# Two halves of a weight in one tile, word by word, and the moving rows at another distance

## The chip, the core and the metric

The kernel runs on one core of a Trainium2 chip, as one launch. The metric is the device time of that launch in microseconds. TensorE (PE in the profile) multiplies, and loads its stationary operand with an instruction of its own (PEld in the profile); VectorE (DVE) and ScalarE (ACT) do the elementwise work, SyncE (SP) issues the transfers of the weights.

## The reference, cut to what matters

Two layer blocks run one after the other on 256 positions of width 2048, in float32. Nearly all of the work is a chain of matrix products with large weights, each weight read once:

```
proj = rmsnorm(h) @ w_in + b_in             # 2048 x 11272, then mLSTM and a causal convolution
h = h + (gates * branches) @ w_out          # 2048 x 2048
u = causal_dwconv(rmsnorm(h) @ w_up)        # 2048 x 11008
h = h + (silu(gate) * val) @ w_down         # 5504 x 2048
# second block, on 16 + 256 positions:
proj = rmsnorm(h) @ w_in_2                  # 2048 x 10240, then pooling, a gated recurrence, gelu
h = h + merged @ w_out_2
h = h + square(relu(rmsnorm(h) @ mlp_w1)) @ mlp_w2   # 2048 x 8192 x 2048
out = rmsnorm(h)
```

## The kernel before, in words

**Products in three parts.** TensorE works here on the type float32r, which keeps fewer bits of a number than float32. So each weight is split in two: a high half (the weight written as float32r, `whi`) and a low half (the weight less its high half, `wlo`). The activations are split in the same way: the tiles `hn` (normalised rows) and `act` (other operands) hold for each of the 16 feature tiles the high part in columns 0 to 255 of the row and the low part behind it. A product of a 128 x 128 block of weights and 256 positions is three matmuls into the same bank of PSUM: high times high, high times low, low times high (L461 to L463). The weights are the stationary operand, the activation rows are the moving one, so each of the three matmuls is preceded by a load of 128 columns of weights.

**The weight stream.** SyncE brings the weights in chunks of 4 x 512 columns per partition (1 MB in all) into a ring `raw` of four. Each chunk is split as two halves of 1024 columns. For each half ScalarE copies raw to a slot of `whi` (L727), VectorE subtracts (L1040) into the same slot of `wlo`, and TensorE runs 24 matmuls on it: 2 rows of tiles, 4 column tiles, 3 parts. There are 4 slots. Half n+4 may be written when the 24 matmuls of half n are done (`half_used`), and the two engines keep their program order three halves ahead (`AHEAD`). All other work of ScalarE and VectorE (moving sums out of PSUM, gates, convolutions, splits of the activations) stands between these splits in an order fixed by hand (`stream`). Everything is ordered by semaphores; there is no scheduler. 952 halves pass through in all.

**The wide stages.** In `lru_in` and `pool_in` of the second block the moving rows are 272 columns (16 extra positions), and the low part comes from the tile `lo2` (L485 to L487, in `group_wide`).

**Where the tiles lie.** The tiles are laid out in each partition in the order of allocation: `raw` (32 KB), `whi` (16 KB), `wlo` (16 KB), `h` (16 KB), an unused `gap_a`, `hn`, `act`, and the rest. A slot of `whi` or `wlo` is 4096 bytes and a block of 128 weights 512 bytes, so every block starts at a multiple of 256 bytes from the start of `whi`. A row of `hn` is 2304 bytes, 9 times 256, and its moving part starts 256 bytes into it; a row of `act` is 2048 bytes. So every moving row of 256 columns starts, modulo 256 bytes, at the same distance from every block of weights: the 192 bytes of `gap_a`. In the wide stages `hn` is read from 64 bytes ahead of that, and the rows of `lo2` are 1088 bytes apart, so that their distance goes through four values.

Of the kernel before, what the change touches and what calls it, by code (L numbers as in the profile page):

```python
# [5 lines left out]
F32R = mybir.dt.float32r  # L6
# [5 lines left out]
P = 128  # L12
# [9 lines left out]
HALF = CK // 2 * NC  # L22
RAW = 4
SLOTS = 4
# [59 lines left out]
def build(nc, a, out):  # L84
    PH, GROUPS, CHUNKS = plan()
    ctx = ExitStack()
    with ctx:
        def sb(name, shape, dt=F32, stack=ctx):
            return stack.enter_context(nc.sbuf_tensor(name, shape, dt))
# [7 lines left out]


        raw = sb("raw", [P, RAW, CK * NC])
        whi = sb("whi", [P, SLOTS, HALF], F32R)  # L100
        wlo = sb("wlo", [P, SLOTS, HALF], F32R)
        h = sb("h", [P, NT, T])

        sb("gap_a", [P, 48])
        hn = sb("hn", [P, NT, MAIN + 2 * T], F32R)
        act = sb("act", [P, NT, 2 * T], F32R)
        meta_lo = hn[:, :, MAIN - 2 * META:MAIN - META]
# [1472 lines left out]
```

How the kernel before makes its waits and increments, by code:

```python
        @block.sync  # L313
# [7 lines left out]
            def load(c, c_slot, dst_cols, src):  # L321
                if not (isinstance(c, int) and c < RAW):
                    sp.wait_ge(lo_ready, 2 * c - 2 * RAW + 2)
                kt, n = src.shape[1], src.shape[2]
                dst = raw[:, c_slot % RAW, :].rearrange("p (k n) -> p k n", n=dst_cols)[:, 0:kt, 0:n]
                sp.dma_start(dst, src).then_inc(chunk_loaded[c_slot % RAW], 16)
# [15 lines left out]
                        load_x(j)  # L343
                    kt = min(CK, w.shape[1] - k0 - CK * j)
                    cl = s * nch + j
                    load(ph.c0 + per_body * i + cl, cl + (body * per_body if ph.unroll else 0), NC,
                         w[:, k0 + CK * j:k0 + CK * j + kt, ds(column, n)])
            for ph in PH.values():
                if ph.name == "lru_gates":
                    for q in range(4):
                        sp.wait_ge(lo_ready, 2 * (ph.c0 + q) - 2 * RAW + 2)
                        for s, w in enumerate((W_ga, W_gx)):
                            sp.dma_start(raw[:, q, s * HALF:(s + 1) * HALF].rearrange("p (k n) -> p k n", n=256),
                                         w[:, 4 * q:4 * q + 4, :]).then_inc(chunk_loaded[q], 16)
# [15 lines left out]
                    c = slice(half * D // 2, (half + 1) * D // 2)  # L372
                    for e in ("even", "odd"):
                        sp.wait_ge(sem(f"out_copied_{e}"), 2 * t + half + 1)
                    sp.dma_start(out[0, t * P:(t + 1) * P, c], out_nat[:, t, c]).then_inc(sem("out_stored"), 16)
```

## Time and profile before

| | us |
|---|---|
| median of 3 runs | 2875.09 (2865.03 to 2888.51) |
| the profiled execution | 2872.45 |
| its span, first to last instruction | 2870.7 |
| TensorE busy in it | 2744.2 (96%) |
| VectorE busy | 1711.4 (60%) |
| ScalarE busy | 1300.1 (45%) |
| mean granted TensorE clock | 0.979 of full speed |

The time is what the launch took on the device; the span is the part of it between the first and the last instruction, here 1.75 us shorter. The profiled execution lies 2.6 us under the median of the runs. TensorE's busy time is the union of overlapping matmuls, so a full share says that it was never without one, not how fast they followed each other.

### The profile page before, as it was taken

Reading aid. Unit: us, or ns where it says so; the run is one execution under the profiler, and the core shown is the slowest. Engines: PE = TensorE matmul, PEld = TensorE weight load, DVE = VectorE, ACT = ScalarE, POOL = GpSimd, SP = SyncE. Lnnn points to the kernel's source line nnn. Section 1 sums busy time; section 2 is a strip of 40 time slices with the busy share of each in tenths; the row PEclk is TensorE's granted clock in tenths of the full one; section 3 lists DMA queues with packets and bytes.
Section 4 is the critical chain, followed back from the end, with each engine's and each line's share of the span. In section 5 each row is a group of like instructions: output and inputs, shape, how many; then the busy total and the mean of one; then the engine's idle time right before and its main releaser. Section 6 shows DMA issues by size and latency. Waiting matters only on the chain.

```text
span 2870.7 us, 53265 instructions
## 1 busy us (share of the span) xinstructions
PE 2744.2 (96%) x22994; PEld 2721.2 (95%) x22994; DVE 1711.4 (60%) x1725; ACT 1300.1 (45%) x1449; POOL 1.8 (0%) x14
## 2 busy tenths in 40 slices
PE   4988999999999999999999967999999999999998
PEld 4987999999999999999989967999999999999998
DVE  4544565566667567657785648755665555455555
ACT  3443454444554355445544375444454334343443
POOL 0000000000000000000000000000000000000000
PEclk9988999999999999999999988999999999999999
DMA  4442555555555555555545424555556565655653
GB/s 154 162 146 93 195 193 192 190 191 191 187 194 180 197 182 196 198 191 165 173 165 171 154 98 132 191 185 182 190 179 189 189 182 187 191 183 185 186 183 115
DMA packets 257814, 503.17 MB, mean 175 GB/s; under 512 B 10150, under 2 KB 19038, under 8 KB 257630
## 3 DMA queue, kind: packets, MB, share of 16 engines
q1 hardware_dynamic: 254592, 500.20, 53.1%
q8 instruction: 127, 2.08, 0.3%
q10 hardware_dynamic: 3054, 0.55, 0.1%
q14 instruction: 41, 0.34, 0.0%
HBM read 498.63 MB, written 2.10 MB: 174 GB/s over the span
## 4 chain that ended last, share of the span: by engine, by line
PE 87%; DVE 7%; ACT 4%; ACTq 1%; issue 1%; DVEq 0%
PE psum L461 27%; PE psum L462 27%; PE psum L463 26%; PE psum L485 2%; PE psum L486 2%; PE psum L487 2%; DVE wlo L1040 2%; DVE work L1068 1%; DVE work L1408 1%; ACT whi L727 1%; ACTq L713 1%; DVE misc L1454 0%; ACT misc L950 0%; DVE hn L1078 0%; DVE work L1439 0%
## 5 line engine op out<-in xcount | busy, mean ns | idle before, releaser
L1040 DVE TENSOR_TENSOR wlo<-raw,whi 128x1024 fp32r<-128x1024 f32 x952 | 1160.1, 1223 | 983.6 <-ACT whi L727 982.7
L727 ACT ACTIVATE whi<-raw 128x1024 fp32r<-128x1024 f32 x952 | 1003.3, 1058 | 1317.4 <-PE psum L463 1194.3
L461 PE MATMUL psum<-hn,whi 128*128 128x256 f32 x4448 | 1249.5, 281 | 38.9 <-DVE wlo L1040 25.9
L462 PE MATMUL psum<-hn,whi 128*128 128x256 f32 x4448 | 1247.0, 280 | 0.0
L463 PE MATMUL psum<-hn,wlo 128*128 128x256 f32 x4448 | 1246.7, 280 | 0.0
L461 PEld LDWEIGHTS psum<-hn,whi 128*128 128x128 f32 x4448 | 846.1, 190 | 42.6 <-DVE wlo L1040 28.9
L463 PEld LDWEIGHTS psum<-hn,wlo 128*128 128x128 f32 x4448 | 848.7, 191 | 0.0
L462 PEld LDWEIGHTS psum<-hn,whi 128*128 128x128 f32 x4448 | 842.5, 189 | 0.1
L461 PE MATMUL psum<-act,whi 128*128 128x256 f32 x2544 | 711.8, 280 | 14.8 <-DVE wlo L1040 9.3
L463 PE MATMUL psum<-act,wlo 128*128 128x256 f32 x2544 | 711.0, 279 | 0.0
L462 PE MATMUL psum<-act,whi 128*128 128x256 f32 x2544 | 710.9, 279 | 0.0
L461 PEld LDWEIGHTS psum<-act,whi 128*128 128x128 f32 x2544 | 479.5, 188 | 16.2 <-DVE wlo L1040 9.9
L463 PEld LDWEIGHTS psum<-act,wlo 128*128 128x128 f32 x2544 | 484.9, 191 | 0.0
L462 PEld LDWEIGHTS psum<-act,whi 128*128 128x128 f32 x2544 | 479.2, 188 | 0.0
L485 PE MATMUL psum<-hn,whi 128*128 128x272 f32 x512 | 150.4, 294 | 6.5 <-DVE wlo L1040 6.5
L486 PE MATMUL psum<-lo,whi 128*128 128x272 f32 x512 | 149.2, 291 | 0.0
L487 PE MATMUL psum<-hn,wlo 128*128 128x272 f32 x512 | 148.6, 290 | 0.0
L485 PEld LDWEIGHTS psum<-hn,whi 128*128 128x128 f32 x512 | 98.1, 192 | 7.2 <-DVE wlo L1040 3.8
L487 PEld LDWEIGHTS psum<-hn,wlo 128*128 128x128 f32 x512 | 98.0, 191 | 0.0
L486 PEld LDWEIGHTS psum<-lo,whi 128*128 128x128 f32 x512 | 98.0, 191 | 0.0
L1053 DVE TENSOR_TENSOR work<-psum,scale 128x1024 f32<-128x1024 f32 (+2 forms) x58 | 70.5, 1215 | 27.2 <-PE psum L463 27.2
L1326 DVE SCALAR_TENSOR_TENSOR work<-work,cols 128x256 f32<-128x256 f32 x172 | 71.9, 480 | 1.7
(207 smaller groups left out, 978.3 us busy)
## 6 DMA issues: line engine op xcount, KB each, us to landing
raw<-in_w_in SPq DMA_DIRECT2D x160, 1024.0 KB, 5.1
raw<-in_mlp_w SPq DMA_DIRECT2D x128, 1024.0 KB, 5.3
raw<-in_w_up SPq DMA_DIRECT2D x80, 1024.0 KB, 5.0
raw<-in_w_down SPq DMA_DIRECT2D x40, 1024.0 KB, 5.1
raw<-in_w_out SPq DMA_DIRECT2D x32, 1024.0 KB, 5.0
raw<-in_w_branch_m SPq DMA_DIRECT2D x8, 1024.0 KB, 5.0
raw<-in_w_branch_c SPq DMA_DIRECT2D x8, 1024.0 KB, 5.0
raw<-in_w_up SPq DMA_DIRECT2D x8, 768.0 KB, 4.4
```

Source lines behind the costliest of these rows:

```text
L461: mm(o, hi[:, kk, w], both[:, 0, :], start=first, stop=False)
L462: mm(o, hi[:, kk, w], both[:, 1, :], start=False, stop=False)
L463: last = mm(o, lo[:, kk, w], both[:, 0, :], start=False, stop=end)
L485: mm(o, hi[:, kk, w], hn[:, kt, MAIN - META:MAIN + T], start=(kt == 0), stop=False)
L486: mm(o, hi[:, kk, w], lo2[:, kt, :], start=False, stop=False)
L487: last = mm(o, lo[:, kk, w], hn[:, kt, MAIN - META:MAIN + T], start=False, stop=(kt == NT - 1))
L713: ac.dma_start(stage[at:at + n, s, :], src).then_inc(sem("stage_loaded"), 16)
L727: A(whi[:, n % SLOTS, :], raw[:, n // 2 % RAW, n % 2 * HALF:(n % 2 + 1) * HALF], ACT.Copy)\
L1040: V.tensor_tensor(wlo[:, n % SLOTS, :], raw[:, n // 2 % RAW, n % 2 * HALF:(n % 2 + 1) * HALF], whi[:, n % SLOTS, :].bitcast(F32), ALU.subt ...
L1053: V.tensor_tensor(dst, summed(ph, i, s, tiles), over_tiles(stream_scale, tiles), ALU.mult)\
L1068: V.tensor_reduce(dst[:, ds(g, 1), :].rearrange("p o t -> p (o t)"), src.rearrange("p k t -> p t k"), AX.X, ALU.add).then_inc(sem("squares ...
L1326: last = V.scalar_tensor_tensor(up_conv[s][:, m, :], up_pad[s][:, m, k:k + T], dcol(f"ffn_w{k}", t), up_conv[s][:, m, :], ALU.mult, ALU.add)
```

## The change

One tile `wsplit` takes the place of `whi` and `wlo`, with 2048 words for each slot. `whi` and `wlo` are now views of it: the high half of weight x is word 2x, the low half word 2x+1. Nothing else in the code is touched, so ScalarE writes every second word, VectorE reads the high halves as every second word and writes the low halves to the words between, and TensorE loads 128 weights from 1024 bytes, every second word of them. The tile begins where `whi` began and takes the same 32 KB. `gap_a` goes from 192 to 64 bytes, so `hn`, `act` and all tiles behind them lie 128 bytes lower, and a moving row of 256 columns starts 64 bytes (modulo 256) from every block of weights. In the wide stages `hn` is read from 0 bytes and `lo2` from other distances than before.

```
-        whi = sb("whi", [P, SLOTS, HALF], F32R)
-        wlo = sb("wlo", [P, SLOTS, HALF], F32R)
+        wsplit = sb("wsplit", [P, SLOTS, 2 * HALF], F32R)
+        whi, wlo = [wsplit[:, :, :].rearrange("p s (x t) -> p s x t", t=2)[:, :, :, t] for t in range(2)]
         h = sb("h", [P, NT, T])
 
-        sb("gap_a", [P, 48])
+        sb("gap_a", [P, 16])
```

The instructions of every engine, their order, their sizes and their waits are the same before and after.

## Rows read from the trace of the kernel before

**Rows 1.** The page: span, TensorE, granted clock in 40 slices, last chain.

```profile
span 2870.7 us, 53265 instructions
PE 2744.2 (96%) x22994; PEld 2721.2 (95%) x22994; DVE 1711.4 (60%) x1725; ACT 1300.1 (45%) x1449; POOL 1.8 (0%) x14
...
PEclk9988999999999999999999988999999999999999
...
PE 87%; DVE 7%; ACT 4%; ACTq 1%; issue 1%; DVEq 0%
```

**Rows 2.** TensorE by stretch: bounds, length, busy (instructions), granted clock, DMA share, GB/s.

```profile
74.00:246.00 172.00, 155.00 (x1172) 0.92 0.39 129
252.00:741.00 489.00, 488.75 (x4306) 1.00 0.58 192
742.00:926.00 184.00, 184.00 (x1564) 1.00 0.56 187
929.00:1357.00 428.00, 427.34 (x3771) 1.00 0.58 190
...
1461.00:1670.00 209.00, 202.46 (x1560) 0.98 0.51 170
...
1792.00:1843.00 51.00, 51.00 (x453) 1.00 0.58 193
1848.00:2859.00 1011.00, 1009.69 (x8567) 1.00 0.57 181
```

**Rows 3.** Timeline of TensorE near 1000 us, the first and last of 28 matmuls.

```profile
999.93 0.28 PE L461 MATMUL psum<-hn,whi 128*128 128x256 f32 x1
...
1002.99 0.28 PE L461 MATMUL psum<-hn,whi 128*128 128x256 f32 x1
```

**Rows 4.** The same near 2000 us, the first and last of 28 matmuls.

```profile
1999.76 0.28 PE L461 MATMUL psum<-hn,whi 128*128 128x256 f32 x1
...
2002.94 0.28 PE L461 MATMUL psum<-hn,whi 128*128 128x256 f32 x1
```

**Rows 5.** The same in a wide stage, the first and last of 25 matmuls.

```profile
1519.90 0.29 PE L485 MATMUL psum<-hn,whi 128*128 128x272 f32 x1
...
1522.92 0.29 PE L485 MATMUL psum<-hn,whi 128*128 128x272 f32 x1
```

**Rows 6.** Timeline of TensorE, 32 matmuls of type float32, one after the other.

```profile
66.81 7.07 PE L540 MATMUL psum<-h,work 128*8 128x256 f32 x32
```

**Rows 7.** Timeline of TensorE at the end, 24 transposes of type float32.

```profile
2856.26 2.85 PE L681 MATMUL psum<-ident,h 128*128 128x128 f32 x24 [1.31 <-DVE h L1293]
```

**Rows 8.** Groups by line: busy us, mean ns of one, idle before, releaser.

```profile
L1040 DVE TENSOR_TENSOR wlo<-raw,whi 128x1024 fp32r<-128x1024 f32 x952 | 1160.1, 1223 | 983.6 <-ACT whi L727 982.7
L727 ACT ACTIVATE whi<-raw 128x1024 fp32r<-128x1024 f32 x952 | 1003.3, 1058 | 1317.4 <-PE psum L463 1194.3 <-PE psum L487 119.6 <-PE psum L646 1.9
...
L1068 DVE TENSOR_REDUCE work<-work 128x256 f32<-128x1024 f32 x24 | 47.9, 2009 | 1.1 <-ACT work L756 1.1
```

**Rows 9.** Who waited for whom: us in total, times, longest us.

```profile
ACT whi L727 <- PE psum L463: 1194.3, 722, 10.2
DVE wlo L1040 <- ACT whi L727: 982.7, 650, 5.8
...
PE psum L461 <- DVE wlo L1040: 35.3, 11, 6.6
```

**Rows 10.** Busy PE, PEld, DVE, ACT, POOL, in an up and an MLP stretch.

```profile
760.00:926.00 166.00, 166.00 (x1411) 166.00 (x1411) 115.01 (x137) 83.88 (x96) 0.00 (x0) 1.00 0.55 184
...
1848.00:2855.00 1007.00, 1006.95 (x8543) 1006.54 (x8542) 565.44 (x494) 415.91 (x405) 0.00 (x0) 1.00 0.57 182
```

**Rows 11.** DMA issues of the page: count, KB each, us to landing.

```profile
raw<-in_w_in SPq DMA_DIRECT2D x160, 1024.0 KB, 5.1
```

## The prediction

> **What bounds the kernel now.** I read the page first. The span is 2870.7 us, TensorE is busy for 2744.2 of it, the granted clock stands at full speed (2.4 GHz) nearly everywhere, and 87% of the last chain is TensorE's own work [rows 1]. In the long stretches it is never idle [rows 2]. The waits say the same from the other side: ScalarE's split waits for TensorE to free a slot for 1194.3 us in all and VectorE's for ScalarE for 982.7 us, while TensorE waited for a low half 11 times, for 35.3 us [rows 9]. So the time is a number of matmuls times the spacing at which they follow each other, and a busy share of 100% hides that spacing. It is the next thing to read.
>
> The timeline gives it. Near 1000 us 27 matmuls take 1002.99 - 999.93 = 3.06 us, 113.3 ns each [rows 3]. Near 2000 us the same instructions at the same clock, on the same tiles, take 2002.94 - 1999.76 = 3.18 us, 117.8 ns each [rows 4]. The counts by stretch show that this isn't a local matter: 252 to 741 us, 929 to 1357 and 1792 to 1843 run at the short spacing (489/4306 = 113.6 ns), 742 to 926 and 1848 to 2859 at the long one (184/1564 = 117.6, 1011/8567 = 118.0) [rows 2]. A stretch keeps its spacing for hundreds of microseconds through stages with other weights and operands, and it changes only where TensorE had to wait. A supply that is too slow would show as idle time and would not stay that even; it looks like the phase between two streams that run side by side, the moving rows and the next weights, which is set when TensorE starts again.
>
> What would be the spacing without such a loss? 32 matmuls in float32, with 256 columns, take (7.07 - 0.38)/31 = 215.8 ns each (0.38 being the last one's own length) [rows 6]. That is two passes of 256 columns at 2.4 GHz (213.3 ns) and 2.5 ns. 24 transposes of 128 float32 columns, each with its own weight load, take (2.85 - 0.27)/23 = 112 ns, the slower first one after the wait included [rows 7]; two passes of 128 are 106.7 ns. So the same array with one load for each matmul comes down to about 106.7 + 2.5 = 109.2 ns, an estimate from these two groups. Against it the three-part product loses 4.1 ns per matmul in one phase and 8.6 in the other. In the wide stage 24 matmuls take 3.02 us, 125.8 ns [rows 5], where 272 columns and 2.5 ns make 115.8: a loss of 10.0 ns, and there the distance of the rows from the weights is another.
>
> **The change part by part.** The instructions are the same, so nothing but the length of one and the spacing can change.
>
> *The weight load and the moving rows.* Before, TensorE reads 1024 bytes of moving row while it reads 512 bytes of weights: the two addresses run at two speeds and one passes the other again and again, modulo whatever length the memory is divided by. After, both walk 1024 bytes in the same 106.7 ns, at a start distance that is 64 bytes (modulo 256) for every pair of `hn` or `act` row and weight block, with low halves only one word off. If the loss comes from the two reads meeting, they can now meet once per matmul at the most and, 64 bytes apart, not at all. I take the loss as gone in the narrow stages: spacing 109.2 ns. The float32 rows are the nearest cases: in [rows 7] both streams also walk at one speed, 512 bytes each, and the loss is small or nil, though at half the rate of bytes, so it is a hint and not a proof. The other end: each block now spans twice the bytes. If meetings go by the bytes that the weight load passes over, the loss doubles, to 113.3 + 4.1 = 117.4 and 117.8 + 8.6 = 126.4 ns.
>
> Sum for the narrow stages: at the short spacing 4306 + 3771 + 453 = 8530 matmuls x 4.1 ns = 35.0 us; at the long one 1172 + 1564 + 8567 = 11303 x 8.6 = 97.2 us [rows 2]. About 1100 more (22994 less these and the 1560 wide ones, less the few hundred of other kinds) stand in the broken stretches between, some 6 us. Together 138 us.
>
> *The wide stages.* 1560 matmuls [rows 2] x 10.0 ns would be 16 us if their loss went too. But here `hn` starts 0 bytes from the weights and `lo2` at four distances, so the even distance doesn't hold. I take half, 8 us, with -16 and +16 us as ends.
>
> *The splits on ScalarE and VectorE.* ScalarE now writes every second word, VectorE reads one source and writes its output so. Bounds: at best nothing changes, 1058 and 1223 ns [rows 8]. The only access in this trace that isn't word after word is the reduction over tiles, which reads 1024 words 1024 bytes apart: 2009 ns, 786 ns over the plain 1024-word subtraction [rows 8]. A hop of 8 bytes is far nearer to 4 than to 1024, so I take 0, and keep 786 ns for one such stream and 1572 ns for two as ends. The cover is large: a half takes TensorE 24 x 113.3 = 2.72 us, there are three halves between a freed slot and its use (8.2 us), and the chain through ScalarE and VectorE is 1.06 + 1.22 = 2.3 us. Doubled it would still fit, as long as VectorE has time on average. That is the point to check. In the up stretch VectorE is busy 115.0 of 166 us for 1411/24 = 59 halves [rows 10]; 59 x 0.786 = 46 more makes 161, above the 59 x 24 x 109.2 ns = 154 us that TensorE would need. In the MLP stretch it is 565 of 1007 us for 356 halves; 280 more makes 845 against 933: it fits.
>
> Two rules of the Trainium skill speak against each other here. The Trainium skill, Vector Engine (DVE) Microarchitecture Reference, section Expressivity limits, says that a stream keeps its full rate only in runs of at least two adjacent 4-byte words, and gives 1.73 ns per column for one source that hops every word and 1.98 for all three; by it a split would take some 1.8 to 2.1 us. The Trainium skill, SBUF — State Buffer, in its remark on 16-byte cachelines, says that two hits in each line of 16 bytes are enough, which every second float32 word gives; by it nothing changes. The page with the price has no case with a hop of 8 bytes, and no row here has one.
>
> *Transfers.* At 109.2 ns a chunk of 1 MB is used up in 48 x 109.2 = 5.24 us, 200 GB/s. The short-spacing stretches already draw 192 at a DMA share of 0.58 [rows 2], a chunk lands 5.1 us after its issue [rows 11], and four are in flight at most. Hidden, cost 0. *Stage borders.* What TensorE waits for there (126 us of span in which it is idle, [rows 1]) is work that starts when its last matmul ends, so it stays; a faster stream leaves a little less cover for it. I put 4 us against the gain.
>
> Sum: 2872 - 138 - 8 + 4 = 2730 us against the profiled execution, which lies 3 us under the median. What a measurement of this kernel can tell from no change is about 1%, 29 us.
>
> **The rivals.**
> (a) *Everything locks at the short spacing.* The meeting costs a fixed part, and only the phase goes: 11303 x 4.5 ns = 51 us, and 2 in the broken stretches: 2819 us. For it: 113.3 is a steady state that the kernel reaches often. Against: it is 4 ns over what float32 does.
> (b) *No contention, no change.* The two spacings come from how the load and the matmul hand over in TensorE's queue, not from the memory: 2872 us, or a few us either way as the phases fall. For it: the spacing is the same for `hn` and for `act`. Against: these have the same distance to the weights, and the wide stage, with another, loses more (10.0 ns). The Trainium skill, SBUF — State Buffer, section Who interferes with whom, states that TensorE has two independent read ports and waits for no one; by this rule the spacing would stay.
> (c) *The loss grows with the span of the weight load* (the other end above): + 138 + 16 us, 3026 us. This is the one that ends slower; it decides as soon as a weight load of 1024 bytes meets the moving row more often than one of 512. For it: twice the bytes are passed over and a low half shares its place with a high one. Against: at equal speed they cannot pass each other.
> (d) *VectorE pays for lone words.* With 786 ns more per split, the up stages (some 22 groups, 490 us) stay at today's pace, 30 us of the gain gone, and some jams behind bursts of other VectorE work, 20 us: 2780 us. With two penalties, 1572 ns, a split is 2.80 us, longer than TensorE's half; then VectorE bounds the kernel: 952 x 2.80 + 551 us of its other work (1711 - 1160) = 3210 us and 60 at the ends, 3270 us.
> (e) *The weight load runs at half rate on every second word.* Each load then takes twice 106.7 ns and sets the spacing at 216 ns or so: + 100 ns x 22994 = 5170 us.
>
> **How the numbers follow.** The forecast, 2700 to 2760 us, gets 0.42: two steady spacings in one kernel are strong evidence of a phase between streams, less strong that the memory is where they meet. (a) 0.12, (b) 0.12, (c) 0.14, (d) 0.06 for 2780 and 0.05 for 3270, (e) 0.06; 0.03 for a loss gone beyond the forecast. Faster by over 1%: 0.42 + 0.12 + 0.06 + 0.01 (b's tail) = 0.61; within 1%: 0.11, rounded 0.12; slower: 0.14 + 0.05 + 0.06 and c's lesser forms, 0.27. The range has to reach (c), as (d)'s upper form, (e) and the low tail already leave out 0.14: 2700 to 3030 us. The likeliest case's own range is 2700 to 2760.
>
> **What would show it.** In the timeline of the changed kernel the spacing of the narrow matmuls should be 109 to 110 ns at 1000 and at 2000 us alike, some 915 matmuls in 100 us in place of 884 and 852; L1040 at 1223 ns and L727 at 1058; the wide ones between 116 and 126 ns. Two spacings still there, at other values, say that the meeting remains (rivals a, c); the same two values, (b). A L1040 of 2 us with TensorE waiting for it in the up stages is (d). PEld longer than 0.19 us with a spacing over 130 is (e). I am wrong if the loss isn't in the memory, or if the weight load cares for the hop.

## The result and the profile after

The changed kernel takes 2968.93 us (median; 2967.76 to 2969.17), the kernel before 2877.2 us on the same chip: ratio 1.033, 95% interval 1.029 to 1.037. It is 3.3% slower, where I had forecast 5% faster. The range of the prediction held it by its upper part, which rival (c) had opened. The profiled execution's span is 2967.4 us, 96.7 us more than before.

The page of the changed kernel, the lines that answer to [rows 1]:

```profile
span 2967.4 us, 53265 instructions
PE 2843.5 (96%) x22994; PEld 2822.6 (95%) x22994; DVE 1720.1 (58%) x1725; ACT 1387.9 (47%) x1449; POOL 1.8 (0%) x14
...
PE 89%; DVE 6%; ACT 3%; ACTq 1%; issue 1%; DVEq 0%
```

TensorE's busy time grew by 99.3 us (2744.2 to 2843.5). Its idle time went from 126.5 to 123.9 us. So the waits as a whole did not grow; the same matmuls follow each other more slowly. TensorE by stretch (columns as in [rows 2]), four windows of 100 us of the changed kernel:

```profile
600.00:700.00 100.00, 100.00 (x836) 1.00 0.53 179
1000.00:1100.00 100.00, 100.00 (x824) 1.00 0.54 174
2000.00:2100.00 100.00, 100.00 (x836) 1.00 0.56 184
2700.00:2800.00 100.00, 100.00 (x824) 1.00 0.58 181
```

A window counts also the two or three matmuls that began before it, so 836 is 100/(836 - 2.5) = 120.0 ns and 824 is 121.7 ns. Two longer stretches of it say the same:

```profile
255.00:740.00 485.00, 485.00 (x4044) 1.00 0.55 183
800.00:1350.00 550.00, 550.00 (x4523) 1.00 0.55 181
```

485/4044 = 119.9 ns and 550/4523 = 121.6 ns. The kernel before had 113.3 and 117.8 ns [rows 3, 4]. There are again two steady spacings; both are longer than either of before. In the wide stage 24 matmuls take 1602.98 - 1599.96 = 3.02 us, to the digit what they took [rows 5]:

```profile
1599.96 0.29 PE L485 MATMUL psum<-hn,wsplit 128*128 128x272 f32 x1
...
1602.98 0.29 PE L485 MATMUL psum<-hn,wsplit 128*128 128x272 f32 x1
```

The groups by line, the ones that answer to [rows 8], and the weight load:

```profile
L1040 DVE TENSOR_TENSOR wsplit<-raw,wsplit 128x1024 fp32r<-128x1024 f32 x952 | 1163.3, 1226 | 1068.6 <-ACT wsplit L727 1066.7
L727 ACT ACTIVATE wsplit<-raw 128x1024 fp32r<-128x1024 f32 x952 | 1091.1, 1150 | 1348.2 <-PE psum L463 1233.0 <-PE psum L487 111.6 <-PE psum L646 1.9
L461 PEld LDWEIGHTS psum<-hn,wsplit 128*128 128x128 f32 x4448 | 884.5, 199 | 40.6 <-DVE wsplit L1040 27.4 <-issue 13.1
```

The weight load in the kernel before:

```profile
L461 PEld LDWEIGHTS psum<-hn,whi 128*128 128x128 f32 x4448 | 846.1, 190 | 42.6 <-DVE wlo L1040 28.9 <-issue 13.3
```

VectorE's subtraction, with one interleaved source and an interleaved output, is where it was (1223 to 1226 ns). ScalarE's copy rose by 92 ns (1058 to 1150) and still waits for TensorE for 1233.0 us, so it costs nothing. The weight load rose from 190 to 199 ns.

The sum closes on the spacings. The changed kernel's mean is about 121.0 ns, between its two spacings. The 8530 matmuls that were at 113.3 ns lose 7.7 ns each, 66 us; the 11303 that were at 117.8 lose 3.2 each, 36 us. Together 102 us, against 99.3 us of busy time and 96.7 us of span.

### The profile page after: what moved, and what is told of

It reads as the page before. It is cut to its first block, busy times and chain, and to the rows that moved or that the text cites. A ratio compares the mean times of both kernels' runs of the same rounds, so it can differ in the third digit from the quotient of the medians.

```text
span 2967.4 us, 53265 instructions
## 1 busy us (share of the span) xinstructions
PE 2843.5 (96%) x22994; PEld 2822.6 (95%) x22994; DVE 1720.1 (58%) x1725; ACT 1387.9 (47%) x1449; POOL 1.8 (0%) x14
## 4 chain that ended last, share of the span: by engine, by line
PE 89%; DVE 6%; ACT 3%; ACTq 1%; issue 1%; DVEq 0%
PE psum L461 27%; PE psum L463 27%; PE psum L462 27%; PE psum L486 2%; PE psum L485 2%; PE psum L487 2%; DVE wsplit L1040 1%; DVE work L1068 1%; ACTq L713 1%; DVE work L1408 1%; ACT wsplit L727 1%; DVE misc L1454 0%; ACT misc L950 0%; DVE hn L1078 0%; DVE work L1439 0%
## 5 line engine op out<-in xcount | busy, mean ns | idle before, releaser
L1040 DVE TENSOR_TENSOR wsplit<-raw,wsplit 128x1024 fp32r<-128x1024 f32 x952 | 1163.3, 1226 | 1068.6 <-ACT wsplit L727 1066.7
L727 ACT ACTIVATE wsplit<-raw 128x1024 fp32r<-128x1024 f32 x952 | 1091.1, 1150 | 1348.2 <-PE psum L463 1233.0
L461 PE MATMUL psum<-hn,wsplit 128*128 128x256 f32 x4448 | 1270.9, 286 | 37.8 <-DVE wsplit L1040 23.9
L462 PE MATMUL psum<-hn,wsplit 128*128 128x256 f32 x4448 | 1268.8, 285 | 0.0
L463 PE MATMUL psum<-hn,wsplit 128*128 128x256 f32 x4448 | 1268.6, 285 | 0.0
L461 PEld LDWEIGHTS psum<-hn,wsplit 128*128 128x128 f32 x4448 | 884.5, 199 | 40.6 <-DVE wsplit L1040 27.4
L462 PEld LDWEIGHTS psum<-hn,wsplit 128*128 128x128 f32 x4448 | 884.4, 199 | 0.0
L463 PEld LDWEIGHTS psum<-hn,wsplit 128*128 128x128 f32 x4448 | 884.0, 199 | 0.0
L461 PE MATMUL psum<-act,wsplit 128*128 128x256 f32 x2544 | 724.9, 285 | 12.0 <-DVE wsplit L1040 7.8
L463 PE MATMUL psum<-act,wsplit 128*128 128x256 f32 x2544 | 724.5, 285 | 0.0
L462 PE MATMUL psum<-act,wsplit 128*128 128x256 f32 x2544 | 724.3, 285 | 0.0
L461 PEld LDWEIGHTS psum<-act,wsplit 128*128 128x128 f32 x2544 | 503.9, 198 | 13.0 <-DVE wsplit L1040 8.4
L463 PEld LDWEIGHTS psum<-act,wsplit 128*128 128x128 f32 x2544 | 503.7, 198 | 0.0
L462 PEld LDWEIGHTS psum<-act,wsplit 128*128 128x128 f32 x2544 | 503.7, 198 | 0.0
L485 PE MATMUL psum<-hn,wsplit 128*128 128x272 f32 x512 | 149.4, 292 | 5.1 <-DVE wsplit L1040 5.1
L486 PE MATMUL psum<-lo,wsplit 128*128 128x272 f32 x512 | 149.4, 292 | 0.0
L487 PE MATMUL psum<-hn,wsplit 128*128 128x272 f32 x512 | 148.6, 290 | 0.0
L485 PEld LDWEIGHTS psum<-hn,wsplit 128*128 128x128 f32 x512 | 100.8, 197 | 5.7 <-DVE wsplit L1040 3.9
L487 PEld LDWEIGHTS psum<-hn,wsplit 128*128 128x128 f32 x512 | 101.4, 198 | 0.0
L486 PEld LDWEIGHTS psum<-lo,wsplit 128*128 128x128 f32 x512 | 101.1, 197 | 0.0
```

The source lines that it names most:

```text
L461: mm(o, hi[:, kk, w], both[:, 0, :], start=first, stop=False)
L462: mm(o, hi[:, kk, w], both[:, 1, :], start=False, stop=False)
L463: last = mm(o, lo[:, kk, w], both[:, 0, :], start=False, stop=end)
L485: mm(o, hi[:, kk, w], hn[:, kt, MAIN - META:MAIN + T], start=(kt == 0), stop=False)
L486: mm(o, hi[:, kk, w], lo2[:, kt, :], start=False, stop=False)
L487: last = mm(o, lo[:, kk, w], hn[:, kt, MAIN - META:MAIN + T], start=False, stop=(kt == NT - 1))
```

## The experiments

Four explanations stood after the result. **Theory A**: the distance of rows and weights decides, and 64 bytes is a bad one. **Theory B**: a weight load of every second word costs TensorE time by itself, at any distance. **Theory D**: the load is slowed by ScalarE and VectorE, which now touch twice the places. And rival (b) of the prediction: the spacing belongs to the hand-over in TensorE's queue.

### Each part of the change alone

*i192*, the interleaved tile with the old gap:

```
-        sb("gap_a", [P, 16])
+        sb("gap_a", [P, 48])
```

> The changed kernel with gap_a back at 192 bytes: halves interleaved word by word, rows 192 bytes from the weights. If the loss comes from where the two reads meet (theory A), the spacing changes with the distance: not 120.0 and 121.7 ns any more, and the time leaves 2969 us by over 1% one way or the other. If a weight load of every second word costs its own time whatever the distance (theory B), the spacing stays at 120 to 122 ns and the time at 2950 to 2985 us.

Measured: 2949.78 us, ratio 1.025 (1.019 to 1.032). The spacing is 120.0 ns throughout.

*s64*, the kernel before with the new gap, `sb("gap_a", [P, 16])`:

> The kernel before with gap_a at 64 bytes: separate tiles for the halves, rows 64 bytes from the weights. Theory A (the distance matters): spacings other than 113.3 and 117.8 ns, and by the changed kernel's result perhaps longer, 2900 to 2970 us. Theory B (only the hop of the weight load matters): 113.3 and 117.8 ns as before, 2860 to 2890 us.

Measured: 2900.28 us, ratio 1.007 (1.004 to 1.010). Three long stretches of it, where [rows 2] has 4306, 3771 and 8567:

```profile
252.00:741.00 489.00, 489.00 (x4154) 1.00 0.57 187
929.00:1357.00 428.00, 427.97 (x3632) 1.00 0.56 185
1848.00:2859.00 1011.00, 1009.96 (x8568) 1.00 0.58 186
```

In the first two the spacing rose from 113.6 and 113.5 to 117.7 and 117.8 ns, the last was there already. So both parts of the change cost: the distance 0.7% by taking the short spacing away, the interleaving (at 192 bytes) 2.5% by lifting everything to 120.0 ns, and with both there is a second value, 121.7 ns. Both theories hold in part; B is the larger.

### Which engine's hop costs

*ld_hop*: ScalarE and VectorE write the halves one behind the other, TensorE alone reads every second word (so it multiplies mixed words). *wr_hop* is the reverse: the two right-hand sides below change places. Both are at 192 bytes. The cut shows ld_hop against the changed kernel, at the first of three places; the other two, the wide stages among them, read `phi` and `plo` in the same way.

```
-        whi, wlo = [wsplit[:, :, :].rearrange("p s (x t) -> p s x t", t=2)[:, :, :, t] for t in range(2)]
+        whi, wlo = [wsplit[:, :, t * HALF:(t + 1) * HALF] for t in range(2)]
+        phi, plo = [wsplit[:, :, :].rearrange("p s (x t) -> p s x t", t=2)[:, :, :, t] for t in range(2)]
...
-                    hi = whi[:, hl % SLOTS, :].rearrange("p (k n) -> p k n", n=NC)
-                    lo = wlo[:, hl % SLOTS, :].rearrange("p (k n) -> p k n", n=NC)
+                    hi = phi[:, hl % SLOTS, :].rearrange("p (k n) -> p k n", n=NC)
+                    lo = plo[:, hl % SLOTS, :].rearrange("p (k n) -> p k n", n=NC)
```

> One half of the change alone, rows 192 bytes from the weights as before: TensorE loads every second word of the one tile, but ScalarE and VectorE write the halves one behind the other, as before, so the products are other numbers. Theory B (the load of every second word costs TensorE its own time): spacing 120.0 ns and a time near 2950 us, as with the whole interleaving at 192 bytes; L727 back at 1058 ns. Theory D (the load is slow because ScalarE and VectorE touch twice as many places of the tile meanwhile): spacing 113 to 118 ns, time near 2875 us.

Measured: 2948.76 us, ratio 1.030 (1.027 to 1.034). The windows of ld_hop at 600 and 1000 us:

```profile
600.00:700.00 100.00, 100.00 (x835) 1.00 0.53 179
1000.00:1100.00 100.00, 100.00 (x835) 1.00 0.55 179
```

ScalarE's copy is back at 1060 ns.

> The other half alone, rows at 192 bytes: ScalarE and VectorE write the halves word by word interleaved, TensorE loads 128 words in a row from the tile, so the products are other numbers. Theory B: spacings 113.3 and 117.8 ns as before, 2865 to 2890 us, L727 at 1150 ns with no effect on the time. Theory D: spacing near 120 ns, near 2950 us.

Measured: 2867.44 us, ratio 0.999 (0.995 to 1.003). The same windows of wr_hop, and its copy on ScalarE (line 728 here):

```profile
600.00:700.00 100.00, 100.00 (x851) 1.00 0.54 183
1000.00:1100.00 100.00, 100.00 (x885) 1.00 0.60 196
```

```profile
L728 ACT ACTIVATE wsplit<-raw 128x1024 fp32r<-128x1024 f32 x952 | 1081.9, 1142 | 1254.2 <-PE psum L464 1138.8 <-PE psum L488 111.9 <-PE psum L647 1.8
```

This pair settles it. TensorE's load of every second word, with nothing else interleaved, gives the 120.0 ns and the 2949 us of i192. The interleaved writes make ScalarE's copy 84 ns longer and leave spacings (117.8 and 113.3 ns) and time where they were. Theory D falls.

*ld_hop4* loads every fourth word in the 256-column stages (`slot[:, m, :, kk]` of `wsplit[:, hl % SLOTS, :]` arranged as "p (m x t) -> p m x t" with t=4; again mixed words):

> As the kernel in which TensorE alone loads every second word, but with every fourth word (16 bytes apart) in the 256-column stages, over the same slot. Theory B with a price by bytes passed over: clearly longer than 120.0 ns, 124 to 135. If each word then needs a fetch of its own, far more, 150 to 216 ns. If the price is for any hop, whatever its length: 120 ns.

Measured once: 5304.42 us. Four weight loads of it, the first and the last:

```profile
999.71 0.33 PEld L462 LDWEIGHTS psum<-hn,wsplit 128*128 128x128 f32 x1
...
1000.41 0.33 PEld L462 LDWEIGHTS psum<-hn,wsplit 128*128 128x128 f32 x1
```

One every 0.23 us, 0.33 us long in place of 0.19. The windows have 427 matmuls, a spacing of 235.6 ns, above every value that I had expected. At 192 bytes a hop of 8 bytes costs 2 to 7 ns of spacing over contiguous loads, one of 16 bytes 118 to 122. This is about the price that rival (e) had put on a hop of 8 bytes; it begins one step further out. A load also spans twice the bytes here, and no run tells that from the longer hop. By the Trainium skill, SBUF — State Buffer, the remark on 16-byte cachelines, two hits per line hold the full rate and a new line for every access does not. The cliff lies where that rule puts it; but at two hits per line the load was not quite at full rate here, at 192 bytes.

### Rows or weights that stand still

In *s_still* (kernel before) and *i_still* (changed kernel, 64 bytes) the moving operand of the 256-column matmuls is one word of its row, read 256 times; in *w_still* and *both_still* (kernel before) the weights are one word, or both are. The products are other numbers.

```
-                            mm(o, hi[:, kk, w], both[:, 0, :], start=first, stop=False)
+                            mm(o, hi[:, kk, w], both[:, 0, 0:1].to_broadcast([P, T]), start=first, stop=False)
```

> The kernel before, with the moving operand of the 256-column matmuls standing still: each reads one word of its row 256 times, so the products are other numbers. The moving read no longer walks. If the loss of 4.1 and 8.6 ns comes from two walking reads that meet, the spacing falls to 109 to 110 ns in all stretches. If it is the hand-over between load and matmul, 113.3 and 117.8 ns stay. If a read that stays on one word is in the way of the weights once in each turn, it could also be longer.

Measured once: 2789.42 us. Windows at 600 and 1000 us:

```profile
600.00:700.00 100.00, 100.00 (x898) 1.00 0.59 200
1000.00:1100.00 100.00, 100.00 (x898) 1.00 0.61 199
```

> The changed kernel with the moving operand of the 256-column matmuls standing still, as in the run beside it. If the weight load of every second word is slow by itself (theory B), the spacing stays near 120 ns and a weight load near 198 ns. If it is slow only because the two reads meet (theory A), 109 to 110 ns and 188 ns.

Measured once: 2905.28 us. The same windows:

```profile
600.00:700.00 100.00, 100.00 (x851) 1.00 0.55 183
1000.00:1100.00 100.00, 100.00 (x851) 1.00 0.56 181
```

> The kernel before with the weights of the 256-column matmuls standing still: each load reads one word 128 times, so the products are other numbers, while the moving rows walk. With the rows standing still instead the spacing was 111.7 ns. If the rest of the loss is the load's walk, the spacing falls to 109 to 110 ns; if a fixed hand-over of the load is in it, it stays at 111 to 113 ns; if only the moving read meets with something else, 113 to 118 ns as before.

Measured once: 2854.93 us; 885 matmuls in the windows at 600, 1000 and 2000 us (113.3 ns), 859 at 2700 us (116.7 ns). Both spacings of the kernel before are still there, the long one 1.1 ns shorter.

> The kernel before with both the weights and the moving rows of the 256-column matmuls standing still, so the products are other numbers. Rows still gave 111.7 ns, weights still 113.3 and 116.7. If all of the loss over 109.2 ns comes from reads that meet or walk, 109 to 110 ns; if a part belongs to the hand-over of the load, 111 to 112 ns or more.

Measured once: 2788.37 us; 898 in the windows at 600 and 1000 us, as in s_still.

Less the 2.5 matmuls that began before the window, 898 is 111.7 ns and 851 is 117.8 ns. The rows that walk are worth 1.6 ns of the short spacing and 6.1 of the long one, and with still rows there was one spacing only. So the walk of the rows costs time, and rival (b), under which nothing in memory matters, falls. The rule cited beside (b), by which the spacing would stay, does not hold here: the spacing moves with the walk of the rows. That it is the weight load that the rows meet is argued, not shown: in w_still the load stays on one word and both spacings remain, so the walk of the load is worth 1.1 ns of the long one and nothing of the short, though a load that reads one word 128 times may still be met. But 111.7 ns stays with both reads still, 2.5 ns over the 109.2 ns that I had taken as the floor: my expectation of 109 to 110 ns failed twice. And with the rows out of the way the interleaved load still gives 117.8 against 111.7 ns. I read these 6 ns as the price of the hop, with no row to meet; i_still and s_still also differ in the gap (64 and 192 bytes), and no pair with still rows has the same one. The length of a load's record does not measure it: it is 194 ns in s_still, at the shortest spacing, and 190 in the kernel before.

### The circle of distances

*s128*, *s0* (gap of 256 bytes), *s224* and *s160* are the kernel before, *i128*, *i0* and *i224* the changed one, each with another size of `gap_a` (in words; s128 is `[P, 32]`).

> The kernel before with gap_a at 128 bytes. At 192 bytes two spacings occur, 113.3 and 117.8 ns; at 64 bytes 117.8 alone. If the distance modulo 256 decides which of them can lock in, 128 bytes gives another mix, 2820 us (113.3 everywhere) to 2905 us (117.8 everywhere); if it is the phase after each wait alone, a mix as before, 2855 to 2890 us.

> The kernel before with gap_a at 256 bytes, so that rows and weights start at the same place modulo 256. If meeting at the start costs, this is the worst of the four distances, over 2905 us and a spacing over 117.8 ns; if only the phase after each wait decides, a mix of 113.3 and 117.8 ns, 2855 to 2890 us.

> The changed kernel with gap_a at 128 bytes. At 64 bytes the spacing was 120.0 and 121.7 ns, at 192 bytes 120.0. If 120.0 ns is the price of the load of every second word and the distance only adds to it, this has 120.0 ns or more, 2945 to 2985 us; if some distance lets the two equally fast reads pass each other, as I forecast for 64 bytes, under 118 ns and under 2900 us.

> The kernel before with gap_a at 224 bytes. Between 192 bytes (113.3 and 117.8 ns) and 256 (120.0 ns): if the grain is 64 bytes, one of these two, 2873 or 2948 us; if it is finer, something between or, if the best distance lies here, 113.3 ns throughout and 2815 to 2830 us.

> The kernel before with gap_a at 160 bytes, between 128 bytes (118.2 to 120.0 ns, 2935 us) and 192. If the grain is 64 bytes, one of these two; if finer, something between, or 113.3 ns throughout and 2815 to 2830 us if the best distance lies here.

> The changed kernel with gap_a at 256 bytes, distance 0. If every interleaved load costs at least 120.0 ns with walking rows, 120 to 123 ns and 2950 to 3000 us. If equally fast reads can pass each other without meeting at some distance, this or the run beside it falls to 117.8 ns (the value with rows that stand still) or less, under 2905 us.

> The changed kernel with gap_a at 224 bytes, a distance that isn't a multiple of 64. If only blocks of 64 bytes count, 120.0 ns as at 192 or as at 0 bytes, near 2950 us. If a finer grain counts, another spacing; by the forecast's idea 117.8 ns or less, under 2905 us.

| distance, bytes mod 256 | separate tiles: us, ratio, matmuls in 100 us at 600 / 1000 / 2000 / 2700 | interleaved: us, the same |
|---|---|---|
| 0 | 2948.52, 1.026 (1.021 to 1.031); 835 / 835 / 835 / 835 | 2956.0 (one execution); 836 / 835 / 835 / 835 |
| 64 | 2900.28, 1.007 (1.004 to 1.010); 852 / 851 / 852 / 851 | 2968.93, 1.033 (1.029 to 1.037); 836 / 824 / 836 / 824 |
| 128 | 2934.72, 1.021 (1.016 to 1.026); 845 / 836 / 845 / 835 | 2965.74, 1.032 (1.027 to 1.037); 828 / 828 / 828 / 836 |
| 160 | 2916.05, 1.018 (1.012 to 1.023); 855 / 836 / 855 / 845 | |
| 192 | the kernel before, some 2875; 885 / 884 / 852 / 851 | 2949.78, 1.025 (1.019 to 1.032); 836 / 835 / 835 / 835 |
| 224 | 2915.47, 1.017 (1.012 to 1.022); 847 / 847 / 847 / 847 | 2951.05 (one execution); 836 / 835 / 836 / 836 |

The ratios are to the kernel before, measured beside each. With separate tiles the distance is worth up to 2.6%, 192 bytes is the best of six, and it is the only one with long stretches at 113.3 ns. The grain is finer than 64 bytes, since 160 (117.3 to 120.0 ns) and 224 (118.4) give values of their own. With the interleaved tile the distance moves the time by less than 1%, no distance is better than 120.0 ns, and 64 (the forecast's) and 128 bytes are the slowest. No version with the right products beats the kernel before.

Two things stand in this table beside that. The price of the hop depends on the distance: 2 to 7 ns at 192, some 2 at 224, and nothing at 0, where contiguous loads have 120.0 ns too. So theory B, which has a price at any distance, holds only in part. And the gap moves the rows while the weights stay where they are, so these runs can't tell the distance between the two from the place of the rows alone.

The wide stages answer to neither part. Some 97 of their matmuls in a row from 1600 us on have 125.7 ns in ld_hop (the load's hop alone), 124.8 in s64, 125.8 in s0 and s128 (the gap alone) and 126.9 in i0. Two matmuls of ld_hop that stand 24 apart:

```profile
1599.98 0.29 PE L486 MATMUL psum<-hn,wsplit 128*128 128x272 f32 x1
...
1602.99 0.29 PE L486 MATMUL psum<-hn,wsplit 128*128 128x272 f32 x1
```

## Why the prediction was wrong

**What held.** The bound (TensorE's spacing, hidden behind a busy share of 100%), that memory is behind the two steady spacings (s_still, the circle; with what the rows meet left open), no cost from the splits (VectorE 1223 to 1226 ns; ScalarE 92 ns, covered), transfers hidden, and waits at the stage borders about the same (126.5 to 123.9 us). Of the two rules weighed for the splits, the one with 1.73 to 1.98 ns per column (the Trainium skill, Vector Engine (DVE) Microarchitecture Reference, Expressivity limits) does not extend to a hop of 8 bytes: 1226 ns for 1024 columns. Rival (d) is out.

**The step that failed** is the first of the parts: "I take the loss as gone in the narrow stages: spacing 109.2 ns". Three things in it were wrong.

The weight load was priced at nothing beside the meeting. I had weighed the hop of 8 bytes for ScalarE and VectorE and, for TensorE, only as rival (e), all or nothing, and as (c), by its span. It has a small price of its own: 120.0 against 113.3 and 117.8 ns with rows that walk at 192 bytes, 117.8 against 111.7 with rows that stand still. That price is paid by every one of some 20,000 narrow matmuls, and alone it is the 2.5 to 3.0% of i192 and ld_hop.

The idea that two reads at equal speed hardly meet was not borne out. The equal speed itself was an assumption: no row shows how fast a load walks its bytes. At 64 bytes the walking rows still cost 2.2 and 3.9 ns (120.0 and 121.7 against 117.8), and at none of five distances was the spacing under 120.0. The hop's price and the loss from the rows don't simply add up: at distance 0 the rows alone make 120.0 ns and the hop adds nothing (s0, i0).

The floor was too low. I took 109.2 ns from float32 matmuls, and the float32r stream of this kernel keeps 111.7 ns with nothing to meet. So even without any loss the narrow stages had some 1.6 and 6.1 ns to give, 14 and 69 us, not 138. A smaller slip: the 0.61 for "faster by over 1%" leaves out the 0.03 for a loss gone beyond the forecast.

**The distance** was taken as harmless by itself. It costs: s64 loses the short spacing, 8530 x 4.5 ns = 38 us by [rows 2], and 20 to 29 us were measured, by the medians and by the profiled executions. The likely reason, not shown, is that in the kernel before the share of the short spacing varies from run to run (2863.76 to 2893.95 us).

**Rival (c)**, "the loss grows with the span of the weight load", gave the sign and 3026 us, 57 too many: it would make 117.4 and 126.4 ns out of 113.3 and 117.8, and the runs show both lifted to nearly the same value. The wide stages, for which it wanted 16 us, did not move (125.8 ns). That the stated range held the result is luck: it reached up for a mechanism that did not act as (c) has it.

**What stays open.** Which of the two spacings a stretch locks to after TensorE has waited is seen and not explained. Nor is it explained why the wide stages feel neither hop nor gap. Without their 16 more columns (6.7 ns at full clock) their 125.8 ns are 119.1, an estimate, near the 120.0 where the hop adds nothing in the narrow stages either; so they may stand at the worst value already. Whether the rows lose time by their distance to the weights or by their own place in memory, no run can tell, as the weights were never moved. What the remaining 2.5 ns over the float32 figure are was not separated.

## What to carry to other kernels

A TensorE that is 100% busy still has a spacing, and two values of it for the same instructions were here a sign that the place of the operands in memory matters: count matmuls in windows of equal length before anything else. Price a changed access pattern for every engine that uses the tile, and first for the one that bounds the kernel; here the writers paid nothing that counts and the weight load paid 2 to 7 ns, 20,000 times. A move that makes two streams run in step is worth a run of each half alone, with one operand standing still, before it is built in.

## What the runs showed of the hardware

- A load of 128 float32r weights from every second word lifts the spacing of 256-column matmuls from 113.3 or 117.8 to 120.0 ns with rows at 192 bytes (ld_hop), and not at all at distance 0 (120.0 in s0 and i0); with still rows it is 117.8 against 111.7 ns. From every fourth word it is some 235 ns (ld_hop4).
- With 272-column matmuls neither the hop nor the gap moved the spacing beyond 124.8 to 126.9 ns.
- With 256-column matmuls and contiguous weights the spacing depends on where the moving rows start, modulo 256 bytes from the weights: 113.3 and 117.8 ns at 192, 117.8 at 64, 118.4 at 224, 117.3 to 120.0 at 160, 118.7 and 120.0 at 128, 120.0 at 0.
- VectorE's subtraction with one source and the output on every second word: 1226 ns for 1223. ScalarE's copy that writes every second word: 1142 to 1161 ns for 1058.
